# Differential attention: the minimum over a row's maxima is taken behind the next score read

## What is computed

```
s1 = einsum('bhqd,bhkd->bhqk', q1b, k1) * scale + bias
s2 = einsum('bhqd,bhkd->bhqk', q2b, k2) * scale + bias
a = softmax(s1) - lam * softmax(s2)
o = einsum('bhqk,bhkv->bhqv', a, v)
```

## Time and profile before

| | |
|---|---|
| median of 3 runs | 2602.57 us (2601.49 to 2603.08) |
| span of the profiled execution | 2600.7 us |
| TensorE busy | 2540.5 us, 98% |
| VectorE busy | 1614.7 us, 62% |
| ScalarE busy | 1212.5 us, 47% |
| differential attention, VectorE's part | 432 to about 773 us of the span |

### The profile page before, as it was taken

One profiled execution on the slowest core, in us unless ns is written; L12 is line 12 of the kernel. 1 busy time (PEld: TensorE's weight loads), 2 busy tenths in 40 slices (PEclk: granted clock), 3 DMA queues, 4 the chain that ended last, 5 costly groups with the idle time before them and its releaser, 6 DMA issues.

```text
span 2600.7 us, 35372 instructions
## 1 busy us (share of the span) xinstructions
PE 2540.5 (98%) x12220; PEld 2114.9 (81%) x12220; DVE 1614.7 (62%) x3499; ACT 1212.5 (47%) x2183; POOL 332.0 (13%) x368
## 2 busy tenths in 40 slices
PE   8999999999999999999999999999999999999997
PEld 7998888777667999977877888888888888888886
DVE  6123306998995776654458677876757465564765
ACT  6112314777764555554544333533335353443554
POOL 1110002222221222210000000000000001111143
PEclk9999999999999999999999999999999999999999
DMA  7334458553332111135677767657655365776787
GB/s 232 122 106 125 126 163 253 143 135 87 93 131 90 36 31 45 41 110 158 194 247 220 221 200 237 218 182 216 190 161 179 110 221 108 171 167 162 203 162 137
DMA packets 329436, 398.59 MB, mean 153 GB/s; under 512 B 21408, under 2 KB 235664, under 8 KB 320944
## 3 DMA queue, kind: packets, MB, share of 16 engines
q1 hardware_dynamic: 311696, 364.41, 44.7%
q0 software_dynamic: 17568, 31.99, 8.4%
HBM read 239.86 MB, written 156.48 MB: 152 GB/s over the span
## 4 chain that ended last, share of the span: by engine, by line
PE 62%; DVE 3%; DMA 1%; ACT 1%; issue 1%; SPq 0%; POOL 0%; DVEq 0%; ACTq 0%; POOLq 0%
PE ff_ps_x L3262 26%; PE ff_ps_m L3262 13%; PE ff_ps_z L3262 6%; PE ml_ps_s L2139 6%; PE ff_ps_m L1695 4%; PE ml_ps_o L2168 4%; PE ml_ps_t L2152 2%; DMA ml_v_raw<-scr_yT 1%; DMA ff_pieces<-scr_acc 0%; PE ff_ps_r L2699 0%; PE mo_ps_t L2716 0%; SPq L2326 0%; DVE ff_pieces L2429 0%; DVE ff_pieces L2620 0%; DVE ff_pieces L2616 0%
## 5 line engine op out<-in xcount | busy, mean ns | idle before, releaser
L3262 PE MATMUL ff_ps_x<-ff_mv_hi_p,ff_st_hi_p 128*128 128x512 f32 x764 | 297.8, 390 | 0.5 <-ACT ff_u L3002 0.5
L3262 PE MATMUL ff_ps_x<-ff_mv_hi_p,ff_st_lo_p 128*128 128x512 f32 x764 | 297.3, 389 | 0.0
L3262 PE MATMUL ff_ps_x<-ff_mv_lo_p,ff_st_hi_p 128*128 128x512 f32 x764 | 297.2, 389 | 0.0
L2139 PE MATMUL ml_ps_s<-wide,ml_qs 128*128 128x416 f32 (+14 forms) x880 | 195.6, 356 | 3.7 <-PEq L137 2.7
L3108 DVE TENSOR_TENSOR ff_st_lo_p<-ff_ps_m,ff_st_hi_p 128x512 fp32r<-128x512 f32 x190 | 130.8, 689 | 103.4 <-ACT ff_st_hi_p L2985 103.4
L2952 POOL DMA_DIRECT2D scr_acc<-ff_pieces x64 | 55.5, 872 | 1015.3 <-DVE ff_pieces L3132 946.9
L3002 ACT ACTIVATE ff_u<-ff_ps_x 128x512 f32<-128x512 f32 x128 | 76.6, 598 | 215.0 <-PE ff_ps_x L3262 215.0
L3262 PEld LDWEIGHTS ff_ps_x<-ff_mv_hi_p,ff_st_hi_p 128*128 128x128 f32 x764 | 143.4, 188 | 32.4 <-issue 2.0
L3262 PEld LDWEIGHTS ff_ps_x<-ff_mv_hi_p,ff_st_lo_p 128*128 128x128 f32 x764 | 143.4, 188 | 29.9
L3262 PEld LDWEIGHTS ff_ps_x<-ff_mv_lo_p,ff_st_hi_p 128*128 128x128 f32 x764 | 143.4, 188 | 29.6
L2139 PEld LDWEIGHTS ml_ps_s<-wide,ml_qs 128*128 128x128 f32 x880 | 152.0, 191 | 16.3 <-issue 2.9
(11 more groups left out here) (318 smaller groups left out, 6349.7 us busy)
## 6 DMA issues: line engine op xcount, KB each, us to landing
st_raw<-in_w_ff SPq DMA_DIRECT2D x64, 512.0 KB, 6.2
scr_hid<-ff_pieces SPq DMA_DIRECT2D x128, 256.0 KB, 2.7
st_raw<-scr_hid SPq DMA_DIRECT2D x64, 512.0 KB, 5.4
ring<-in_w_ff SPq DMA_DIRECT2D x28, 1024.0 KB, 7.7
scr_t<-ring SPq DMA_DIRECT2D x24, 1024.0 KB, 5.8
ring<-scr_t SPq DMA_DIRECT2D x21, 1024.0 KB, 8.1
scr_acc<-ff_pieces POOLq DMA_DIRECT2D x64, 256.0 KB, 4.1
ring<-scr_u SPq DMA_DIRECT2D x13, 1024.0 KB, 8.4
```

What stands on the lines that cost most here:

```text
L2139: m = pe.matmul(ps_s[n % NSB][:, 0:w], q, k, start=j == 0, stop=j == len(pairs) - 1)
L3262: m = pe.matmul(bank[:, :], w[kind][:, k], a[kind][:, k], start=start and k == 0 and i == 0, stop=stop and k == KH - 1 and i == 2, skip_gr ...
```

## The change

The minimum leaves `chunk` and becomes a step of its own, "max", which VectorE alone handles (`row_max`). `row_steps` puts it in `later` with one chunk to pass, just ahead of "exp". Its instruction, its operands and its wait for `scores_read` stay as they were.

```diff
@@ row_steps
                         later = [(left, step) for left, step in later if step[2] - NT * step[1] >= i]
-                        later.append((1, ("exp", 0, i, c)))
+                        later += [(1, ("max", 0, i, c)), (1, ("exp", 0, i, c))]
                         if c == 0:
                             later.append((SCALE_AFTER, ("scale", 0, i)))
@@ chunk, on VectorE
-                if k0 + w == META + P * (i + 1):
-                    dve.wait_ge(scores_read, NCH * h + n + 1)
-
-                    dve.tensor_scalar(nmax_all[:, 0:nth + 1], mx[:, i % 2, c, 0:nth + 1], -scale, None, ALU.mult, ALU.min,
-                                      accum_out=nmax[:, i % 2, c:c + 1]).then_inc(max_ready, 1)
                 if first_head and n == 1:
                     lambda_sums()
+
+            def row_max(h, i, c, **at):
+                n = max(m for m in range(NCH) if chunks[m][:2] == (i, c))
+                parts = sum(1 for chunk in chunks if chunk[:2] == (i, c))
+                dve.wait_ge(scores_read, NCH * h + n + 1)
+
+                dve.tensor_scalar(nmax_all[:, 0:parts], mx[:, i % 2, c, 0:parts], -scale, None, ALU.mult, ALU.min,
+                                  accum_out=nmax[:, i % 2, c:c + 1]).then_inc(max_ready, 1)
@@
-            heads(dve, {"chunk": chunk, "scale": invert, "end": end})
+            heads(dve, {"chunk": chunk, "max": row_max, "scale": invert, "end": end})
```

## The result

| | before | after |
|---|---|---|
| median | 2601.49 us (5 runs, 2598.54 to 2603.08) | 2665.95 us (5 runs, 2665.15 to 2670.25) |
| span of the profiled execution | 2600.7 us | 2663.8 us |
| ratio to before | | 1.0258, 95% interval 1.0247 to 1.0269 |

The kernel became 2.6% slower, 64.5 us by the medians. The forecast was 2664 us, with 2643 to 2690 as range.

The account below looks back on a forecast made before the run. Bound by VectorE in the attention stage, TensorE close behind; -15.4 + 59 + 35 - 9.2 - 2.8 - 5 = +61.6 us on the 2600.7 us span, with 1.9 us around it 2664 us; 80% range 2643 to 2690.

Parts of the forecast that it names:

- What bounds the stage: Differential attention, 432 to 773 us: VectorE leads with 29.1 us idle, TensorE follows closely, ScalarE's exponentials hardly show.
- The wait removed, -15.4 us: At 128 minima on VectorE, the 0.12 us wait for the row's last maximum goes: -15.4 us.
- "scale", +59 us: "scale" waits for row (i, 0)'s exponential, no longer covered by "end": 0.92 us mean, 64 times.
- "end", +35 us: "end" waits for row (i, 1)'s exponential: 25.8 us for blocks 0 to 14, 9.0 for block 15, over four heads.
- the old 9.2: VectorE's earlier waits for ScalarE's exponentials, 6.7 and 2.5 us, contained in the new waits and taken off: -9.2 us.
- the 0.04 us that the prediction gave a chunk "to start": In the "scale" wait, 0.04 us added to the 0.49 us of the one chunk beside the exponential.
- What the waits replace: VectorE's old waits: -9.2 us for exponentials, -2.8 for GpSimd at "end", -5 of 8.4 for scores.
- The sum: Whole kernel: -15.4 + 59 + 35 - 9.2 - 2.8 - 5 = +61.6 us, giving 2664 us.
- The clock: Rival, chance 0.06: TensorE's clock falls for a third of its 330 us of work, +98, 2701 us; forecast kept 1.00.
- The rival of a gain: Chance 0.04: no new wait arises at the chunk behind the minimum, TensorE's bank waits shrink: -15.4, 2587 us.

Follow-up runs that it names:

- the kernels with the cover given back: The change plus "end" of the block before moved behind the next chunk and minimum: 2607.53 us; with its added wait at "scale" 2606.88; change of heads as before 2609.74.
- every version with `put_off`: Kernels putting "end" of the block before one chunk later: with minima moved 2607.53, 2606.88 and 2609.74 us; "end" alone, in the kernel before, 2601.72 us.
- the kernel with the wait at "scale": The change with "end" also one chunk later, and the additional wait for the earlier "end" at "scale" instead of at a chunk: 2606.88 us, ratio 1.0018.

## Why the prediction was right, point by point

- **What bounds the stage.** VectorE leading with TensorE close behind it was right in the direction that mattered. More work on VectorE lengthens the stage (15.4 us for 29.2 of added instructions), less work hardly shortens it (-2.9 us, 0.9991, with some 10 us taken from VectorE's busy and idle time together, though 5.6 of them went into new waits for ScalarE). The text had one lead where there are nearly two; with the new waits VectorE's lead became so large that it made no difference to the forecast.
- **The wait removed, -15.4 us.** By the trace -15.1. The rule of the Trainium skill ("VectorE: DVE Perf Modes", "The DRAIN you can't avoid"), by which a wait between chained instructions costs nothing extra, is not borne out for an instruction that needs the last result: 0.12 us in 128 places, 0.00 where it no longer needs it. For a wait on something long finished it agrees: 64 of them more, 0.9993. (The prediction counts four instructions in the earlier trace rows that follow an accumulator read without a gap; there are three, at 586.07, 589.14 and 589.75.)
- **"scale", +59 us.** The profile shows 56.9 us of idle time in 64 waits, and 1.46 us at block 14 where 1.49 was worked out. The step from start to start is longer than the idle time by the 0.08 us of the accumulator read ahead of it, 5 us in 64.
- **"end", +35 us.** The profile shows 31.9 us, 55 waits. Both terms together, less the old 9.2, were to be 84.8 us; the steps into reciprocals grew by 88.6. Some 4 us too low. The term that was mis-sized is the 0.04 us that the prediction gave a chunk "to start": in the trace after, the chunk behind a minimum starts with its accumulator read (both at 618.69), and 0.04 us in 124 places is 5 us. ScalarE started 0.12 us behind that read, as assumed, in 124 of 128 places, and 0.57 us later in three.
- **What the waits replace.** GpSimd's 2.8 us went, 2.6 by the steps. The waits for scores fell by 4.2 us in the profile's count and by 8.6 in the steps to a chunk, where I took off 5.
- **The sum.** +61.6 against +64.5 us is closer than its terms: 4 us too little for the exponentials, 3.6 too little taken off for scores, and 2 us of small steps that were not in it. That the first two cancel is luck; the mechanism and the place of every large term are not.
- **The clock.** It did fall, against what I wrote: about 42 us of the stage at the lower level, 1.2 instead of 2.4 GHz, in eight stretches, and a mean of 0.95. Four of them begin in or right behind waits of TensorE for "end" at a change of heads, of 3.15 to 4.67 us; the others behind waits of 0.9 to 2.0 us. It was not the rival that I priced: it would have decided above a fifth of TensorE's work, and 42 of 410 us is about a tenth. VectorE's waits for scores, which would be its price, were 4.2 us in all.
- **The rival of a gain.** It needed ScalarE to be through by the time "scale" comes. It was not, in any of the 64 places. What it would have been worth is not shown: the kernels with the cover given back came out 6 to 10 us slower than the kernel before, but they still leave row (15, 0) without cover.

That gap in the timeline of TensorE after, and then two windows around it: TensorE was busy 1.16 of 3.5 us at the full clock, and had about half the clock in the next 6.8.

```profile
536.24 1.09 PE L1645 MATMUL da_ps_t<-ident,da_rows 128*128 128x128 f32 x8 [3.15 <-DVE da_rows L1579]
```

```profile
533.90:537.40 3.50, 1.16 (x10) 1.17 (x11) 3.16 (x10) 0.59 (x3) 0.01 (x1) 1.00 0.00 0
537.40:544.20 6.80, 5.07 (x17) 3.66 (x16) 4.27 (x26) 4.58 (x13) 1.18 (x3) 0.51 0.01 4
```

## What to carry to other kernels

A step moved "behind the next read" also moves behind everything else that the list puts out at that place; here that was the longest instruction of the block, and it had been the cover of another engine's longest one. Ask of a moved release what stood beside the released work before, and what stands there now: the wait is the path less that, summed over the places, and this sum came out within 3 us. Then look whether the schedule has a place where a step comes due by another rule: here the fifth chunk of one row left it uncovered in every version with `put_off`. And where two engines are nearly full, time taken from one can come back as its waits, while time added to it counts: here 9.9 us less gave 2.9 us, and 29.2 us more cost 15.4.

## What the runs showed of the hardware

- A small VectorE instruction that waits for the result of the one ahead starts 0.12 us after that one's accumulator read starts; one that waits for something long finished starts with it, 0.00 us. 64 additional waits of the second kind changed neither the time (0.9993) nor the steps from an accumulator read to a chunk (12.3 us both times).
- TensorE's clock went to the lower level inside a stage in which TensorE was busy 88% of the time, in or behind waits of 0.9 to 4.7 us. The length of the wait alone does not decide it: in the kernel with the wait at "scale", the same wait of 1.9 us at block 15 came with the lower level in two of three heads. About 42 us at that level in the kernel after left VectorE waiting 4.2 us for scores, less than the 8.4 us before: TensorE was not what that stage waited for.
